# State-space tiles in six row buffers with conditioning weights streamed in 1 MB steps, and the row rotation moved behind the last tile

## What is computed

```python
ada = cond @ ada_w + ada_b                       # 1024 x 6144, conditioning
h = rms_norm(x, mix_pre_g) * (1.0 + sc_m) + sh_m
proj = h @ w_in
u_s, q, k, v, g_s, g_a = jnp.split(proj, splits, axis=-1)
# state-space branch: 32 groups of 64 states
bu = jnp.einsum('gpc,bsgc->bsgp', b_bar, ug)
_, states = lax.associative_scan(_linear_recurrence, (a, bu), axis=1)
y = jnp.einsum('gcp,bsgp->bsgc', c_mat, states).real + d_skip * uf
y = gelu(y); y = y * sigmoid(y @ w_glu)
q, k = apply_rope(q, positions), apply_rope(k, positions)
```

## Time and profile before

| | before |
|---|---|
| median of 3 runs | 2422.41 us (2419.97 to 2429.88) |
| the profiled execution's own time | 2422.49 us |
| its span in the profile | 2420.4 us |
| TensorE busy | 2221.8 us, 92% of the span |
| VectorE / ScalarE / GpSimd busy | 960.2 / 605.2 / 27.4 us |
| mean granted TensorE clock | 0.971 of full |

### The profile page before, as it was taken

One profiled execution on the slowest core, in us unless ns is written; L12 is line 12 of the kernel. 1 busy time (PEld: TensorE's weight loads), 2 busy tenths in 40 slices (PEclk: granted clock), 3 DMA queues, 4 the chain that ended last, 5 costly groups with the idle time before them and its releaser, 6 DMA issues.

```text
span 2420.4 us, 26402 instructions
## 1 busy us (share of the span) xinstructions
PE 2221.8 (92%) x10794; PEld 1292.1 (53%) x10794; DVE 960.2 (40%) x1683; ACT 605.2 (25%) x991; POOL 27.4 (1%) x44
## 2 busy tenths in 40 slices
PE   5888987999999899989975999989999999999998
PEld 3336842333333333333321888556887887555887
DVE  6782132222222222221213555344555554363655
ACT  2103020110101001001101443344434443154443
POOL 0010000000000000000000000000000000100000
PEclk9999989999999999999987999989999999999999
DMA  7534239999999999999997344224543453412541
GB/s 312 205 143 187 109 119 428 427 423 428 428 427 422 427 428 420 427 428 427 420 428 333 149 164 184 111 88 157 209 165 160 196 208 113 157 66 105 194 171 79
DMA packets 40765, 633.64 MB, mean 262 GB/s; under 512 B 4800, under 2 KB 4800, under 8 KB 5728
## 3 DMA queue, kind: packets, MB, share of 16 engines
q1 hardware_dynamic: 40640, 631.90, 63.4%
HBM read 630.84 MB, written 1.05 MB: 261 GB/s over the span
## 4 chain that ended last, share of the span: by engine, by line
PE 68%; DMA 18%; DVE 3%; ACT 2%; issue 1%; SPq 0%; ACTq 0%; DVEq 0%
DMA piece<-in_moe 18%; PE bank L1768 10%; PE bank L1684 10%; PE bank L1686 9%; PE bank L1685 9%; PE bank L599 6%; PE bank L1803 5%; PE bank L1218 3%; PE bank L1181 2%; PE bank L1749 2%; PE bank L1827 2%; PE bank L1013 1%; PE bank L1185 1%; PE bank L2088 1%; PE bank L1022 1%
## 5 line engine op out<-in xcount | busy, mean ns | idle before, releaser
L1768 PE MATMUL bank<-piece,xeT 128*64 128x512 f32 (+1 forms) x2304 | 453.1, 630 | 73.9 <-DMA piece<-in_moe 70.9
L1690 DVE TENSOR_TENSOR ffn_lo<-slot,ffn_hi 128x2048 fp32r<-128x2048 f32 x132 | 302.1, 2292 | 170.7 <-ACT ffn_hi L2213 165.1
L1768 PEld LDWEIGHTS bank<-piece,xeT 128*64 128x64 f32 (+1 forms) x2304 | 136.3, 133 | 357.9 <-issue 331.7
L1684 PE MATMUL bank<-ffn_hi,hT_hi 128*128 128x512 f32 x704 | 280.6, 399 | 8.4 <-DVE hT_lo L523 6.0
L2213 ACT ACTIVATE ffn_hi<-slot 128x2048 fp32r<-128x2048 f32 x132 | 251.7, 1913 | 130.2 <-PE bank L1686 115.2
L1686 PE MATMUL bank<-ffn_hi,hT_lo 128*128 128x512 f32 x704 | 275.5, 391 | 0.0
L1685 PE MATMUL bank<-ffn_lo,hT_hi 128*128 128x512 f32 x704 | 274.8, 390 | 0.0
L1875 DVE TENSOR_TENSOR hT<-hT,bank 128x512 f32<-128x512 f32 x144 | 92.2, 683 | 271.1 <-PE bank L1827 264.8
L599 PE MATMUL bank<-slot,hT 128*128 128x512 f32 (+1 forms) x384 | 169.2, 590 | 0.0
L1922 DVE TENSOR_SCALAR work<-bank 128x256 f32<-128x256 f32 x60 | 25.5, 425 | 355.2 <-PE bank L1775 355.2
L1684 PEld LDWEIGHTS bank<-ffn_hi,hT_hi 128*128 128x128 f32 x704 | 132.7, 189 | 38.1 <-issue 8.5
(11 more groups left out here) (610 smaller groups left out, 2336.9 us busy)
## 6 DMA issues: line engine op xcount, KB each, us to landing
piece<-in_moe SPq DMA_DIRECT2D x192, 2048.0 KB, 25.4
slot<-in_ffn SPq DMA_DIRECT2D x44, 3072.0 KB, 10.4
slot<-in_ada SPq DMA_DIRECT2D x6, 3072.0 KB, 10.0
slot<-in_merge SPq DMA_DIRECT2D x4, 3072.0 KB, 13.7
slot<-in_nsa_in SPq DMA_DIRECT2D x5, 2048.0 KB, 7.5
slot<-in_w_in SPq DMA_DIRECT2D x4, 2048.0 KB, 9.0
slot<-in_ada SPq DMA_DIRECT2D x3, 2560.0 KB, 9.0
slot<-in_hy_in SPq DMA_DIRECT2D x3, 2048.0 KB, 7.7
```

The costliest lines, as they stand in the source:

```text
L1684: pe.matmul(out, left[0], right[0], start=start, stop=False)
L1690: return dve.tensor_tensor(lo, x, hi.bitcast(F32), ALU.subtract)
L1768: pe.matmul(bank[n * c:n * (c + 1), :], x[:, kt, :], w[i][:, at:at + 512], start=kt == 0, stop=False)
```

## The change

- The loop order. VectorE makes the tables of quads 0, 1 and 2 ahead of tile 0 (quad 1 before `ada_vector` of group 0), that of quad 3 between tiles 2 and 3, with slot 2's upper third as scratch. Tile 0 waits for six tables (`trig_done` >= 6).
- Six row buffers (`ssm_rows`): the two of `ssm_r` and two each in columns 4096 to 6143 of slots 1 and 2. `outputs` runs once per quad, its 16 matmuls ordered so that four successive ones go to four different 32-partition groups.
- Conditioning and projection in parts. The conditioning product is cut in 16 steps of one row tile (1 MB, `ada_step_tensor`), one per state tile, from three thirds of slot 0; bias and gains are 0.5 MB parts of their own. The projection weights come as six halves of 1 MB in two thirds of slot 2, and `project` does three matmuls per tile.
- The row rotation: VectorE's follows tile 15, its last skip, the last `ada_vector` and the last projection copy; GpSimd's waits for `table_free` >= 4, the end of tile 15. The last GELU stands ahead of broadcasts 4 to 7 on ScalarE.
- The names of three pairs of semaphores are merged (`rows_dve`, `rows_pool`), with counts raised to fit.

```diff
@@ -195,16 +202,33 @@
...
-    item("ssm_b", ("ssm_b", 0), 4096, (sig["bu_ready"], SSM_TILES), slot=1)
-    item("w_qkv0", ("w_in", 1), 4096, (sig["proj_ready"], 4), slot=2)
-    ada(3, 0)
-    item("w_qkv1", ("w_in", 2), 4096, (sig["proj_ready"], 6), slot=2)
-    ada(4, 0)
-    ada(5, 0)
-    ada(6, 0)
-    item("w_qkv2", ("w_in", 3), 4096, (sig["proj_ready"], 8), slot=2)
-    ada(7, 0)
-    ada(8, 0)
+    item("ssm_b", ("ssm_b", 0), 4096, (sig["ssm_y_ready"], SSM_TILES // SSM_Q), slot=1)
+    sems = {(0, 0): sig["slot0"], (0, 1): sig["ada_landed1"], (0, 2): sig["ada_landed2"], (2, 0): sig["slot2"], (2, 1): sig["qkv_landed"]}
+    held = {(0, 0): freed[0], (0, 1): freed[0], (0, 2): freed[0], (2, 0): freed[2], (2, 1): freed[2]}
+    count = {at: landed[at[0]] if at[1] == 0 else 0 for at in sems}
+    def part(name, src, lo, width, slot, sub, done):
+        count[slot, sub] += 16
+        plan[name] = Part(src, lo, width, slot, 2048 * sub, held[slot, sub], sems[slot, sub], count[slot, sub])
+        order.append(plan[name])
+        held[slot, sub] = done
+    def qkv(h):
+        part(f"qkv{h}", ("w_in", 1 + h // 2), 2048 * (h % 2), 2048, 2, h % 2, (sig["qkv_half"], h + 1))
+    def ada_step(i):
+        g, kt = divmod(i, KT)
+        n = next(p for p in range(3) if kt in ADA_PARTS[p])
+        part(f"step{i}", ("ada", 3 * (g + 1) + n), ADA_GROUP * ADA_PARTS[n].index(kt), ADA_GROUP, 0, (i + g) % 3, (sig["ada_ready"], 3 + i + 1))
+    def ada_tail(g):
+        part(f"tail{g}", ("ada", 3 * g + 2), 2 * ADA_GROUP, 2 * 512, 0, (9 * g - 1) % 3, (sig["ada_rows"], g + 1))
+    for what in ("q0 q1 s0 s1 s2 s3 s4 s5 q2 s6 s7 t1 q3 s8 s9 q4 s10 s11 s12 s13 q5 s14 s15 t2").split():
+        {"q": qkv, "s": ada_step, "t": ada_tail}[what[0]](int(what[1:]))
+    for slot in (0, 2):
+        landed[slot] = count[slot, 0]
+    freed[0], freed[2] = (sig["ada_rows"], 3), (sig["qkv_half"], 5)
...
@@ -304,13 +328,31 @@
...
+def ada_step_tensor(k, pe, i):
+    s = k["sig"]
+    g, kt = divmod(i, KT)
+    it = k["plan"][f"step{i}"]
+    bank = k["ps"][g]
+    pe.wait_ge(it.sem, it.landed)
+    for c in range(4):
+        at = it.at + c * 512
+        mm = pe.matmul(bank[32 * c:32 * c + 32, :], k["cond"][:, KT + kt:KT + kt + 1].to_broadcast([P, 32]), k["ring"][it.slot][:, at:at + 512], start=kt == 0, stop=kt == KT - 1)
+    mm.then_inc(s["ada_ready"], 1)
...
-    it = k["plan"][f"ada{3 * g + 2}"]
+    if g == 0:
+        it, at = k["plan"]["ada2"], 2 * ADA_GROUP
+    else:
+        it = k["plan"][f"tail{g}"]
+        at = it.at
+        dve.wait_ge(it.sem, it.landed)
...
-    bias, gain = (k["ring"][it.slot][:, 2 * ADA_GROUP + i * 512:2 * ADA_GROUP + (i + 1) * 512] for i in range(2))
-    dve.wait_ge(s["ada_ready"], 3 * g + 3)
+    bias, gain = (k["ring"][it.slot][:, at + i * 512:at + (i + 1) * 512] for i in range(2))
+    dve.wait_ge(s["ada_ready"], 3 + KT * g)
...
@@ -781,7 +823,13 @@
...
-    scratch = k["ssm_r"][:, :, :, :, :].rearrange("p a b c d -> p a (b c) d") if q % 2 == 0 else k["rows"][:, 0:2 * D].rearrange("p (a b d) -> p a b d", a=2, b=SSM_Q)
+    if q == 1:
+        scratch = k["rows"][:, 0:2 * D]
+    elif q == 3:
+        scratch = k["ring"][2][:, 4096:6144]
+    else:
+        scratch = k["ssm_r"][:, :, :, :, :].rearrange("p a b c d -> p (a b c d)")
+    scratch = scratch.rearrange("p (a b d) -> p a b d", a=2, b=SSM_Q)
     return scratch[:, 0, :, :], scratch[:, 1, :, :]
...
@@ -791,6 +839,15 @@
...
     act.activation(k["table"][:, q, 0, :, :], b, ACT.Sin, scale=-TURN, bias=k["quarter"][:, 0:1]).then_inc(s["trig_done"], 1)
+def ssm_rows(k, j):
+    i = j % SSM_ROWS
+    if i < 2:
+        return k["ssm_r"][:, i, :, :, :]
+    at = 4096 + 1024 * (i % 2)
+    return k["ring"][i // 2][:, at:at + 1024].rearrange("p (a b c) -> p a b c", a=2, b=2)
...
@@ -799,8 +856,8 @@
...
         q, jj = divmod(j, SSM_Q)
-        if j == 0:
-            dve.wait_ge(s["trig_done"], 8)
+        if jj == 0:
+            dve.wait_ge(s["trig_done"], 6 if q == 0 else 8)
         cosb = spread(k["table"][:, q, 0, jj, :], 2)
...
@@ -817,9 +874,9 @@
...
         vs.wait()
-        if j >= 2:
-            dve.wait_ge(s["ssm_y_ready"], j - 1)
-        R = k["ssm_r"][:, j % 2, :, :, :]
+        if j >= SSM_ROWS:
+            dve.wait_ge(s["ssm_y_ready"], (j - SSM_ROWS) // SSM_Q + 1)
+        R = ssm_rows(k, j)
         vs.mark(dve.tensor_tensor(R[:, 0, :, :], B[:, :, :], cosb, ALU.mult))
...
@@ -833,7 +890,7 @@
...
     s = k["sig"]
-    dve.wait_ge(s["ssm_y_ready"], 4 * q + 4)
+    dve.wait_ge(s["ssm_y_ready"], q + 1)
     lo = PARAM_AT["d_skip"][0]
...
@@ -854,38 +911,47 @@
...
-    def outputs(j):
-        q, jj = divmod(j, SSM_Q)
-        if jj == 0 and q >= 2:
+    def outputs(q):
+        if q >= 2:
...
-        if j == 0:
+        if q == 0:
...
-        pe.wait_ge(s["rotated"], j + 1)
-        out = k["ps"][6 + q % 2][32 * jj:32 * jj + 32, 0:S]
-        R = k["ssm_r"][:, j % 2, :, :, :]
+        pe.wait_ge(s["rotated"], SSM_Q * (q + 1))
...
-            mm = pe.matmul(out, k["c_mix"][:, c, 32 * j:32 * j + 32], R[:, trig, part, :], start=n_ == 0, stop=n_ == 3)
+            for jj in range(SSM_Q):
+                j = SSM_Q * q + jj
+                mm = pe.matmul(k["ps"][6 + q % 2][32 * jj:32 * jj + 32, 0:S], k["c_mix"][:, c, 32 * j:32 * j + 32], ssm_rows(k, j)[:, trig, part, :], start=n_ == 0, stop=n_ == 3)
...
-    def project(lo, hi):
-        project_tensor(k, pe, ["w_qkv0", "w_qkv1", "w_qkv2"], 2, [512] * 3, k["hT"], KT, 2, range(lo, min(hi, 6 * KT)), (2, 3))
+    def project(m):
+        j, at = divmod(m, 2 * KT)
+        half, t, kt = at // KT, at // 4 % 2, at // KT * 4 + at % 4
+        it = k["plan"][f"qkv{2 * j + half}"]
+        u = 2 + 2 * j + t
+        if at % KT == 0:
+            pe.wait_ge(it.sem, it.landed)
+        if kt == 0 and j >= 1:
+            pe.wait_ge(s["proj_act"] if t == 0 else s["proj_dve"], j + 1)
+        lo = it.at + (kt % 4) * 512
+        mm = pe.matmul(k["ps"][2 + u % 2][:, :], k["hT"][:, kt, t * P:(t + 1) * P], k["ring"][it.slot][:, lo:lo + 512], start=kt == 0, stop=kt == KT - 1)
+        if kt == KT - 1:
+            mm.then_inc(s["proj_ready"], 1)
+        if at % KT == KT - 1:
+            pe.drain().then_inc(s["qkv_half"], 1)
...
-    project(0, 2 * KT)
...
-        if j in (1, 3, 5, 8, 10, 12):
-            ada_tensor(k, pe, 3 + (1, 3, 5, 8, 10, 12).index(j))
-        if 2 <= j < 8:
-            project(16 + 3 * (j - 2), min(16 + 3 * (j - 1), 32))
-        elif j >= 10:
-            project(32 + 3 * (j - 10), 32 + 3 * (j - 9))
-        if j in (7, 9, 11, 13):
-            ada_wide_tensor(k, pe, (j - 7) // 2)
-        outputs(j)
+        for m in range(3 * j, 3 * j + 3):
+            project(m)
+        if j >= SSM_Q and j % SSM_Q == 0:
+            outputs(j // SSM_Q - 1)
+        if 10 <= j < 14:
+            ada_wide_tensor(k, pe, j - 10)
+        ada_step_tensor(k, pe, j)
+    outputs(SSM_TILES // SSM_Q - 1)
...
@@ -3122,6 +3189,9 @@
...
                     name, i = it.src
+                    if isinstance(it, Part):
+                        sp.dma_start(k["ring"][it.slot][:, it.at:it.at + it.width], src[name][i, :, it.lo:it.lo + it.width]).then_inc(it.sem, 16)
+                        continue
                     sp.dma_start(k["ring"][it.slot][:, 0:it.width], src[name][i, :, 0:it.width]).then_inc(k["landed"][it.slot], 16)
...
@@ -3164,19 +3234,17 @@
...
-            act.wait_ge(s["trig_done"], 8)
...
-            ada_wide_scalar(f, act, 0)
...
-            for i in range(1, 4):
+            for i in range(4):
...
+            gelu_scalar(f, act, 3)
...
-            gelu_scalar(f, act, 3)
...
@@ -3252,33 +3320,33 @@
...
             ssm_angles(f, dve, 0)
+            ssm_angles(f, dve, 1)
             ada_vector(f, dve, 0)
...
             first_norm_vector(f, dve)
-            ssm_angles(f, dve, 1)
             ssm_mix_vector(f, dve)
             dve.drain().then_inc(s["ssm_prep_dve"], 1)
+            ssm_angles(f, dve, 2)
             k["vs"].mark(dve.tensor_copy(k["mask_b"][:, 0, :], con(k, "causal")))
...
             dve.tensor_copy(f["uT"][:, 2:4, :].rearrange("p a b -> p (a b)"), k["ps"][1][:, :]).then_inc(s["proj_dve"], 1)
-            ssm_angles(f, dve, 2)
+            ssm_vector(f, dve, range(0, 3))
             ssm_angles(f, dve, 3)
-            ssm_vector(f, dve, range(0, 2))
+            ssm_vector(f, dve, range(3, 6))
             project_read(f, dve, 1, 2, qkv_dst, (0,), (2, 3))
-            ssm_vector(f, dve, range(2, 6))
+            ssm_vector(f, dve, range(6, 9))
             ada_vector(f, dve, 1)
-            ssm_vector(f, dve, range(6, 9))
+            ssm_vector(f, dve, range(9, 11))
             project_read(f, dve, 1, 2, qkv_dst, (1,), (2, 3))
+            ssm_vector(f, dve, range(11, 16))
+            ssm_skip(f, dve, 3)
+            ada_vector(f, dve, 2)
+            project_read(f, dve, 1, 2, qkv_dst, (2,), (2, 3))
             dve.wait_ge(s["proj_dve"], 3)
...
```

(50 more changed lines are left out.)

16 lines of the change are left out of this document (8 added, 8 removed).

## The result

| | before | after |
|---|---|---|
| median | 2424.34 us (4 runs, 2419.97 to 2429.88) | 2393.91 us (4 runs, 2388.18 to 2395.96) |
| ratio, 95% interval | | 0.9872 (0.9848 to 0.9897) |
| profiled execution: its own time, span | 2422.49, 2420.4 us | 2393.53, 2391.5 us |
| transposes of q and k start | 197.3 us | 169.1 us |
| first expert transfer issued | 346.7 us | 319.0 us |

The kernel is 30.4 us faster by the medians and 28.9 us by the two spans; 27.1 were forecast. Of the 28.9, 28.2 are there when the transposes start and 27.7 when the first expert transfer goes out, so the stages behind pass the gain on. Measured a second time, the ratio was 0.9889 (0.9871 to 0.9908).

A forecast was written before the change was run, and what follows sets the result against it. TensorE was taken to bind the loop where it carries conditioning or projection, VectorE elsewhere. 15.4 us from tile 0's start plus 18.5 from the loop less 6.8 in the tail gave 27.1 off 2422.5: 2395 us, range 2390 to 2402.

The forecast's parts named there:

- Step 1: Start of the state-space stage: with angles moved into VectorE's 7.12 us gap, tile 0 starts at 58.6, 15.4 us earlier.
- Step 2: VectorE's chain from tile 0 to tile 15: operations sum to 89.4 us, so tile 15 ends at 148.0 instead of 181.9.
- Step 3: TensorE feeding the loop: 4.82 us a tile against VectorE's 4.88, quads 1.7 us each, 86 of 89.4 us needed.
- serial quads: Rival on the loop's outputs: 16 matmuls don't overlap, 7.4 us a quad, transposes at 192, time 2417 us; chance 0.07.
- Step 4: Weight transfers during the loop: parts land before they are needed, cost 0, spare 3.7 us at the tightest, step 10.
- Step 5: Tail behind tile 15: grows from 15.4 us, with broadcasts at half clock and collision 1.7 us; transposes at 170.2.
- the loss of 0.5 us a tile: Rival in the loop: TensorE takes the bound through handovers or half clock, 8 us more, 2403 us; chance 0.10.
- the rival of half clock: In the loop, TensorE pauses in each tile and its clock stays at 1.2 GHz: about 2470 us; chance 0.03.
- the last rival: At the loop's start, tile 0 still waits for something that ends near 74: 2410 us; chance 0.02.

The follow-up runs named there:

- e9: Kernel before with only quad 1's angles moved ahead of the first bias and gain: 2423.33 us against 2424.11, ratio 1.000 (0.9986 to 1.0014).
- e2: Changed kernel with quad 3's angles ahead of tile 0 again instead of between tiles 2 and 3: 2389.78 us, transposes at 168.8 us.
- e5: Changed kernel with VectorE's rotation ahead of tile 11 instead of behind tile 15: transposes at 172.8 us, 113.7 us behind tile 0.
- e1: Changed kernel with a quad's 16 matmuls in the old order, four of one tile one behind the other: 2405.33 us, ratio to before 0.9933.
- e10: Changed kernel with GpSimd's rotation also waiting for the bias and gains of group 2: 2395.43 us, transposes at 168.1 us.
- e4: Changed kernel with GpSimd's rotation waiting for two quads instead of four, so it runs in the loop: 2396.01 us, transposes at 173.0 us.

## Why the prediction was right, point by point

- **Step 1** forecast tile 0 at 58.6; it was at 58.36. The explanation was weaker than the number: filling the gap alone is worth nothing (`e9`), and tile 0's start isn't a gain of its own (`e2`). "15.4 from tile 0's start, 18.5 from the loop" adds up rightly, but the split means little: the 7.2 us of quad 3's angles can stand on either side of it.
- **Step 2** forecast the end of tile 15 at 148.0; it was 147.99. The sum of VectorE's operations carried the forecast, and `e5` shows that 4.0 us more in it delay tile 15 by 4.1.
- **Step 3**, TensorE against VectorE, a near tie: step 15 of the conditioning was forecast to end at 149.4 and ended at 148.5. A quad took 1.86 (1.7). The stall at tile 3 was 4.62 us (3.8), and `inputs` behind it took 2.07 us, about twice the 1.06 that I summed; with the projection's 3.17 behind them instead of 2.58 the half clock cost 1.6 us (1.8):

```profile
81.54 2.07 PE L911 MATMUL bank<-uT,slot 128*128 128x256 f32 x4 [4.62 <-DVE work L866]
```

  The bound of 7.4 for serial quads was a mis-sized term: 4.6, and 2405 instead of 2417.
- **Step 4**, the transfers: a 1 MB part of the conditioning landed in 5.1 us (4.8), one of the projection in 7.1 (medians between 55 and 150 us), and no matmul waited. The part for step 10, called the tightest, went out at 112.31 (112.4).
- **Step 5**, the tail: 21.1 us from the end of tile 15 (22.2). The quad came 1.1 us sooner than forecast, the collision cost the bias and gains 1.4 us (1.7), and the broadcasts took 6.4 us (5.6), 2.6 more than at full clock where I took 1.8. These misses have opposite signs, so that the total is 1.1 us off and not more is in part luck. The 1.8 came from one stall; after stalls of 2.66 to 4.25 us the runs show a loss between nothing and 2.7 us, so this term has no fixed size.
- **The rivals.** TensorE and VectorE tie, and the loss of 0.5 us a tile didn't come. Nor did the pauses in each tile on which the rival of half clock rested: TensorE stands still for 0.8 of the 62 us at a granted clock of 1.00, so that rival fell by its condition and its mechanism wasn't put to a test. Half clock followed the two stalls of 4.62 and 4.09 us. The Trainium skill, TensorE: Matmul & The Clock Gate, section "A second HAM failure mode: psum-queue depth-cycling", speaks of pauses between groups of matmuls; for the same reason no row of this loop is for or against it. A slip in the chances: the last rival's 2410 lies just outside the 0.5% (down to 2410.3) within which it was counted; it had 0.02, and nothing hangs on it.
- The medians moved by 30.4 where the stage moved by 28.2. The spans differ by 28.9, and executions of one kernel by up to 8 us, so the rest is within what the runs vary; it wasn't followed up.

## What to carry to other kernels

Sum what the carrying engine must do between two fixed points, here from the copy of u to the last tile, and ask of each edit whether it takes work out of that stretch, fills an idle part of it, or only moves work within it; only the first two pay, and an idle gap ahead of the stretch pays only when the work put in it makes room for work of the stretch to go ahead of it. When work is moved behind a loop, read the new order of the tail as closely as the loop: here the stall it left cost twice, once as idle time and once as half clock. Where a chain of waits runs over one engine, look at the busy time of the next one and add a little work to it before calling it free: here both carried the loop.

## What the runs showed of the hardware that was not expected

- Matmuls of 32 columns written one tile behind the other overlap in part when they follow directly: 32 records in 4.6 us, against 1.84 us for 8 with other work between the tiles and 1.86 us for 32 in the four-way order.
- The length of a stall doesn't tell what the clock costs behind it. The same four broadcasts, 3.8 us at full clock, took 6.39 us in one execution of the changed kernel and 5.30 in another, behind stalls of 4.09 and 3.96 us. Over all runs they took 5.26 to 6.49 us behind stalls of 3.96 to 4.25, and behind stalls of 2.66, 2.68 and 2.68 they took 5.43 (`e1`), 5.40 (`e10`) and 3.86 us (`e4`). What decides it wasn't found.

```profile
154.52 5.30 PE L400 MATMUL bank<-work,consts 128*128 128x512 f32 x8 [3.96 <-DVEq L366]
```

- VectorE and GpSimd each took about 1.7 us for an operation of 128 x 512 with two SBUF inputs when both had a queue of them, against 0.69 and 1.27 alone.
